# Value products of 64-feature heads over 128 columns, rings of PSUM banks begun anew in each stage, weaving words chosen anew

## The reference, cut to what matters

```python
def chunk_causal_softmax_attention(q, k, v, scale):          # 16 heads, v has 64 features
    ...
        sc = jnp.einsum('bhqd,bhkd->bhqk', qb, k).astype(jnp.float32) * scale
        sc = jnp.where(chunk_causal_mask(q_pos, k_pos), sc, -jnp.inf)
        p = jax.nn.softmax(sc, axis=-1)
        return jnp.einsum('bhqk,bhkd->bhqd', p.astype(v.dtype), v)

def stick_breaking_attention(q, k, v, scale):                # 8 heads of 64
    ...
        w = jnp.where(strict, jnp.exp(log_beta + later), 0.0)
        return jnp.einsum('bhqk,bhkd->bhqd', w.astype(v.dtype), v)

def _nsa_mixer(h, pos, pos_k, pos_v, wk1, wk2, wv1, wv2):    # 8 heads of 64, 2 groups of keys and values
    ...
    o_slc = _selected_attention(q, ks, vs, idx, pos)
    o_win = _window_attention(q, kw, vw)
    o = gt[..., 0:1] * o_cmp + gt[..., 1:2] * o_slc + gt[..., 2:3] * o_win
```

## Time and profile before

| | |
|---|---|
| median of three runs | 2344.5 us |
| the profiled execution: its own time, its span | 2355.76 us, 2354.0 us |
| ScalarE, GpSimd busy | 1109.1 us (47%), 421.9 us (18%) |
| TensorE weight loads busy | 1973.6 us (84%) |
| chain that ended last, share of TensorE | 89% |
| mean granted clock of TensorE | 0.969 |
| HBM | 306.89 MB read, 131 GB/s over the span |

### The profile page before, as it was taken

How to read it: one execution, slowest core, us unless ns; L and a number is a source line. 1 busy time by engine, 2 the same in 40 slices (tenths; PEclk the granted TensorE clock), 3 DMA queues, 4 the chain that set the end, 5 groups by cost and what they waited for, 6 DMA issues and landing times.

```text
span 2354.0 us, 36461 instructions
## 1 busy us (share of the span) xinstructions
PE 2240.2 (95%) x14254; PEld 1973.6 (84%) x14254; DVE 1534.3 (65%) x2717; ACT 1109.1 (47%) x2003; POOL 421.9 (18%) x377
## 2 busy tenths in 40 slices
PE   6999999999999999999999998999998898999997
PEld 5888889888888878998889886888888786788886
DVE  5976755587688668567765784457765675436765
ACT  4654454365465443535544333346544432235554
POOL 2421001122122100023200230002222140001223
PEclk9999999999999999999999999899998899879999
DMA  6554432255555543125544212124553311203552
GB/s 236 192 179 165 144 108 100 79 185 180 191 188 184 186 143 108 37 87 185 184 180 155 96 48 74 46 72 178 190 177 117 116 48 39 81 9 126 188 178 92
DMA packets 88732, 310.31 MB, mean 132 GB/s; under 512 B 9840, under 2 KB 12144, under 8 KB 88048
## 3 DMA queue, kind: packets, MB, share of 16 engines
q1 hardware_dynamic: 88272, 305.29, 36.6%
q10 hardware_dynamic: 288, 2.69, 0.3%
HBM read 306.89 MB, written 1.05 MB: 131 GB/s over the span
## 4 chain that ended last, share of the span: by engine, by line
PE 89%; DVE 5%; ACT 3%; issue 2%; POOL 1%; DMA 0%; SPq 0%; DVEq 0%; ACTq 0%; POOLq 0%
PE ps L140 87%; PE ps L145 2%; DVE scratch L165 2%; ACT scratch L154 1%; DVE w_lo L165 1%; ACT w_hi L154 1%; POOL scratch L165 1%; DVE x L165 0%; ACT scratch L191 0%; DVE scratch L192 0%; DVE stats L182 0%; DMA ring<-in_w 0%; ACT L159 0%; ACT h L154 0%; DVE scratch L177 0%
## 5 line engine op out<-in xcount | busy, mean ns | idle before, releaser
L165 DVE TENSOR_TENSOR w_lo<-ring,w_hi 128x1024 fp32r<-128x1024 f32 (+2 forms) x571 | 697.2, 1235 | 427.1 <-ACT w_hi L154 421.7
L140 PE MATMUL ps<-h,w_hi 128*128 128x512 f32 (+1 forms) x2784 | 871.6, 372 | 30.2 <-DVE h L177 19.1
L154 ACT ACTIVATE w_hi<-ring 128x1024 fp32r<-128x1024 f32 (+2 forms) x571 | 581.5, 1032 | 491.7 <-PE ps L140 484.9
L140 PE MATMUL ps<-h,w_lo 128*128 128x256 f32 x2448 | 687.8, 281 | 0.0
L140 PEld LDWEIGHTS ps<-h,w_hi 128*128 128x128 f32 x2784 | 505.7, 191 | 128.9 <-issue 26.6
L140 PEld LDWEIGHTS ps<-h,w_lo 128*128 128x128 f32 x2448 | 465.9, 190 | 0.0
L140 PE MATMUL ps<-f,w_hi 128*128 128x512 f32 (+1 forms) x1444 | 420.6, 357 | 2.6 <-DVE f L165 2.6
L140 PE MATMUL ps<-f,w_lo 128*128 128x256 f32 x1184 | 332.5, 281 | 0.0
L165 POOL TENSOR_TENSOR f<-f_work,f 128x256 fp32r<-128x256 f32 x132 | 188.2, 1426 | 598.0 <-ACT f L154 597.9
L140 PEld LDWEIGHTS ps<-f,w_hi 128*128 128x128 f32 x1444 | 256.3, 191 | 45.1 <-DVE w_lo L165 3.1
L140 PE MATMUL ps<-scratch 64*128 64x128 f32 (+10 forms) x1952 | 271.5, 311 | 18.1 <-DVE scratch L165 10.7
(11 more groups left out here) (136 smaller groups left out, 2223.8 us busy)
## 6 DMA issues: line engine op xcount, KB each, us to landing
ring<-in_w SPq DMA_DIRECT2D x520, 512.0 KB, 3.3
ring<-in_w SPq DMA_DIRECT2D x48, 384.0 KB, 3.5
ring<-in_w SPq DMA_DIRECT2D x16, 396.0 KB, 5.6
stage_consts<-in_ctwo ACTq DMA_DIRECT2D x1, 1344.0 KB, 5.8
stage_consts<-in_cthree ACTq DMA_DIRECT2D x1, 1281.0 KB, 5.4
ring<-in_w SPq DMA_DIRECT2D x9, 128.0 KB, 2.5
stage_consts<-in_cone SPq DMA_DIRECT2D x1, 1083.0 KB, 5.8
x<-in_x SPq DMA_DIRECT2D x4, 256.0 KB, 4.1
```

The source lines that it names most:

```text
L140: return self.e.matmul(out, lhsT, rhs, start=start, stop=stop, skip_group_check=free)
L154: return self.e.activation(out, x, func, **k)
L165: return self.e.tensor_tensor(out, a, b, op)
```

## The change

It has three parts.

1. The value products of heads with 64 features take 128 columns of values: the 64 that are wanted and 64 beside them (the other head of a pair, the other group, or the keys that lie next to the values). VectorE reads only the wanted half. This is in m0 (8 stick-breaking heads), m1, b0 and b1 (16 units each): 168 matmuls go from 128x64 to 128x128.
2. `K.cursor.clear()` at the start of each stage: every ring of banks begins at its first bank.
3. New words. Those of c0, c1, m0 and m1 are letter for letter as before. In b0 the 192 working pieces keep their order, two z are gone and a few have moved. In b1 the working pieces stand in another order, and there are 235 z where there were 252.

Of the dummies in the words, those issued are 230 in b0 (232 before), 217 in b1 (225) and 85 in c1 (91); in m0, m1 and c0 as many as before.

```diff
 WEAVE = {
...
-    "b1": ("zzzzzzzzzrrzzrgrrrhlrzzzzzrzzzzzzggzzhzzhzzzzzhrrhzzzhhzzzzzzzzzzzzzzzzzzzhzzzzhzzzzzzzzzrzhrzzh"
...
+    "b1": ("zzzzzzzzzrzrrrrzrgghzgrrhhhzlzzzzzzzzrzhzzzzzzzrhgzzhzhzzzzzzzzzzzrzzzzzrhhlrhzrzrzhrlzzzzzhhrzr"
...
 class Attn:
-    def __init__(self, K, name, lanes, q, k, v, dv, mask, bufs, stats, ready, values):
+    def __init__(self, K, name, lanes, q, k, v, dv, mask, bufs, stats, ready, values, col=None):
...
+        self.col = col or (lambda u: 0)
...
-                ins = e.mm(b[:, 256 * q:256 * q + A.dv], A.p(u)[:, c:c + 128], A.v(u, k), k == 0, k == n - 1)
+                ins = e.mm(b[:, 256 * q:256 * q + 128], A.p(u)[:, c:c + 128], A.v(u, k), k == 0, k == n - 1)
...
-            ins = sink(q, b[:, 256 * q:256 * q + A.dv], st[:, 4 + q:5 + q])
+            c = 256 * q + A.col(u)
+            ins = sink(q, b[:, c:c + A.dv], st[:, 4 + q:5 + q])
...
-        v = lambda k: T.vb[:, k, 64 * h:64 * h + 64]
+        v = lambda k: T.vb[:, k, 128 * (h // 2):128 * (h // 2) + 128]
...
-        e.mm(b[:, 0:64], l[:, 0:128], v(0), True, True)
+        e.mm(b[:, 0:128], l[:, 0:128], v(0), True, True)
...
-                      lambda u, k: self.c[:, k, 128 * u + 64:128 * u + 128], 64, "chunk", bufs,
+                      lambda u, k: self.c[:, k, 128 * u:128 * u + 128], 64, "chunk", bufs,
...
-                       lambda u, k: self.kk[:, k, 2 * (1 + u % 2) + 1, u // 8, :], 64,
+                       lambda u, k: self.kk[:, k, 2 * (1 + u % 2) + 1, :, :].rearrange("p g d -> p (g d)"), 64,
...
 def pe_program(e, K):
     e.wait_ge(K.S.sem("loaded_c"), 16)
     for name, T, order in stages(K):
+        K.cursor.clear()
         for what, i in order:
```

More of the change, by code:

```diff
@@ L40 @@
 WEAVE = {
[L41 to L45, removed]
-    "b1": ("zzzzzzzzzrrzzrgrrrhlrzzzzzrzzzzzzggzzhzzhzzzzzhrrhzzzhhzzzzzzzzzzzzzzzzzzzhzzzzhzzzzzzzzzrzhrzzh"
[L47 to L50, removed]
+    "b0": ("zzzzzzzzzzrrrrrrglrzzrzhgghhzhzzzzzzrzrhzzzzzzzzzzzzzzzzzhzzzzzzzzzzzzzhzzzzzzzzzzzzrhzzzzzzzhzh"
+           "rhhlzzzzzzrzzhrrhrgszzzzzzzhrzzzzhzshzzlhshrzszzhshrrhzznzzzzzzzzzzzzzzzzrzrzzzzzzzzzzzznzzznzzz"
+           "zzzzzzzznnzznznnrvzznrrrnzzzzrwzzzzzzszzrzzzzrnzzzzvwrzzzzzzzzzzszzzzzzzzzrzzznrzrsrnzursnuzrszz"
+           "zzzzrnnsuwvwsrsvsrurrrzwuzvzrururvzrvmwruwvuruvwrvwzrzvzzzuwzuuvzwvzuwwvuuwzvzumzwummmzzzzzmzzzz"
+           "zmmmmmmzzmzmmmzmmmmzzmzzzmzmmzmmzzzzzzzzzzmmmzzzzmzzmzzmzzmzzzzmmzz"),
+    "b1": ("zzzzzzzzzrzrrrrzrgghzgrrhhhzlzzzzzzzzrzhzzzzzzzrhgzzhzhzzzzzzzzzzzrzzzzzrhhlrhzrzrzhrlzzzzzhhrzr"
+           "zzzzzzzszzzzzzhzzzzzzhzrzrszzzrzhszzzhsshzrsrhrhzrzzhzzzzzzzzzzzszzzrzzzzzzzznzrzsznrsnrznzzzzzz"
+           "znzznzzwzrzzzzzznzzzznrzzsrzrnzrszrzzsrznwzzzzzzzzzzzzzzsrzzrzznvzzzzszzzzzzzzzzruzzzzzzzrzzznzz"
+           "znnrzvrnrnrwuzrurwurvuwvumrvuvrvzwrzzzzzzzzvuwuuzvwvuwwvuuwvvzuwwvuuzwzvumwummzmzmzzmmmmmmzzzmmz"
+           "zmmmzzmzmmmmmzzmmzmmzmzzmmzzzmzzmmzzzmzzmzz"),
     "c0": ("zzzzzzzzzpppzzzzpzzzzzzzzzzzzzzzzzzzzzzzzzzzzzzzzzzzzzzzzzzzpzpazcbacdbzacdbdozozzzozoozoozzozoo"
@@ L1555, in pe_stick @@
             e.wait_ge(*K.at("evicted", ((T.stage, "lvb"), t)))
-        e.mm(b[:, 0:64], l[:, 0:128], v(0), True, True)
-        e.mm(b[:, 256:320], l[:, 128:256], v(0), True, False)
-        e.mm(b[:, 256:320], l[:, 256:384], v(1), False, True).then_inc(*e.up("weighted", ("stick", h)))
+        e.mm(b[:, 0:128], l[:, 0:128], v(0), True, True)
+        e.mm(b[:, 256:384], l[:, 128:256], v(0), True, False)
+        e.mm(b[:, 256:384], l[:, 256:384], v(1), False, True).then_inc(*e.up("weighted", ("stick", h)))
 def act_mixer0(e, K, T, what, i):
@@ L1680, in dve_stick @@
         e.wait_ge(*K.at("weighted", ("stick", h)))
-        b = K.psum(("stick", h, "o"))[:, :].rearrange("p (t n) -> p t n", t=2)[:, :, 0:64]
+        b = K.psum(("stick", h, "o"))[:, :].rearrange("p (t n) -> p t n", t=2)[:, :, 64 * (h % 2):64 * (h % 2) + 64]
         e.cp(T.mix[:, :, 512 + 64 * h:576 + 64 * h], b).then_inc(*e.up("evicted", ("stick", h, "o")))
@@ L1726, in __init__ @@
         self.A = Attn(K, stage, 3, lambda u: self.qT[0:96, u, :], lambda u: self.kT[0:96, u, :],
-                      lambda u, k: self.c[:, k, 128 * u + 64:128 * u + 128], 64, "chunk", bufs,
+                      lambda u, k: self.c[:, k, 128 * u:128 * u + 128], 64, "chunk", bufs,
                       [K.st[:, 64 + 8 * i:72 + 8 * i] for i in range(3)],
-                      lambda u: [K.at("evicted", ((stage, n), u // 2)) for n in ("qT", "kT")], lambda u: [])
+                      lambda u: [K.at("evicted", ((stage, n), u // 2)) for n in ("qT", "kT")], lambda u: [], lambda u: 64)
     def chains(self):
@@ L2056, in __init__ @@
                        lambda u: self.kT[1 + u % 2][rows(u // 2), u // 8, :],
-                       lambda u, k: self.kk[:, k, 2 * (1 + u % 2) + 1, u // 8, :], 64,
+                       lambda u, k: self.kk[:, k, 2 * (1 + u % 2) + 1, :, :].rearrange("p g d -> p (g d)"), 64,
                        "causal", bufs, [K.st[:, 64 + 8 * i:72 + 8 * i] for i in range(3)],
                        lambda u: [K.at("evicted", ((stage, "nqT"), u // 8)), K.at("evicted", ((stage, "nkT", 1 + u % 2), 0))],
-                       lambda u: [])
+                       lambda u: [], lambda u: 64 * (u // 8))
     def block_of(self, what, i):
```

## The result

| | before | changed |
|---|---|---|
| median of the runs, on one chip | 2343.35 us | 2306.94 us |
| the profiled execution: its own time, its span | 2355.76 us, 2354.0 us | 2309.56 us, 2307.8 us |
| mean granted clock of TensorE | 0.969 | 0.980 |

The ratio of the runs is 0.9836, with a 95% interval of 0.9809 to 0.9863. The change is faster by 1.6%, about 38 us. One of the changed kernel's four executions took 7535.05 us at a mean granted clock of 0.369; it is in the median above but not in the ratio, and the median of the other three is 2304.33 us. The forecast was 2319.7 us with a range of 2306 to 2338: the direction was right, the gain was half as large again, and those three have their median just under the range.

A forecast was written before the change was run, and what follows sets the result against it. The prediction took TensorE, in its order and at the clock it is granted, as the bound. Its terms summed to -24.8 us, taken off the median of 2344.5 to give 2319.7 us, with a range from 2306 to 2338.

The forecast's parts named there:

- Value products, +3: 168 matmuls made twice as wide: nearly free but for group edges, a cost of 3 us.
- Rival 4: Value products: width sets the spacing, so they cost 19 us instead of 3; 2335.9 us, chance 0.05.
- Rings, -3.1, -2 and -0.7: Rings begun anew: f1's whole wait goes (-3.1 us), b0's start gains 2, six fewer dummies in c1 gain 0.7.
- The words, -8: b1's new order covers TensorE's 6.71 us wait for gate factors; 8 us saved, bounds -18 and +7.
- The clock in b1's last units, -11: Wide products end or prevent the 30 us at 1.2 GHz in b1's last attention units, saving 11 us.
- rival 1: b1's 30 us at low clock belong to the profiled execution alone; only -13.8, 2330.7 us, chance 0.22.
- The clock in b0, -3: In b0, 22 records at low clock: the clock rises earlier there, saving 3 us (0 and -5).
- f1's start: f1's first matmul was to follow c0's last dummy without idle time.
- b0's two pieces: The idle time before b0 was to be shorter than 3.68 us and broken in two.
- the 6.71: TensorE's 6.71 us wait for VectorE's gate factors in b1's first part, which was to go.

The follow-up runs named there:

- e19: The changed kernel measured once more, on another chip than its first runs: 2308.9 us.
- e1: The kernel before with the wide value products alone, rings and words as before: 2341.2 us.
- e8: The changed kernel with b1's new word used in b0 too, wide products: 2293.8 us.
- e13: Narrow value products, rings begun anew, and b1's new word in both b0 and b1: 2291.3 us.
- e11: e4's kernel with ring ATT starting one bank further at b1 (bank 4 first), as in the kernel before: 2335.2 us.
- e4: The changed kernel with the old word of b1: 2325.5 us.
- e2: The kernel before with the rings begun anew at each stage, narrow products and old words: 2347.0 us.
- e7: The kernel before with only ring ATT begun anew, at b1 alone: 2348.2 us.
- e5: e4's kernel with one letter of b1's old word moved, so that piece gl stands right behind gx: 2327.5 us.
- e10: The changed kernel with b1's new word up to piece gl and the old word from there on: 2322.9 us.
- e14: e10's kernel with the RWKV matrices and first inverse step of the first half of tokens ahead of the second half's: 2326.6 us.
- e15: e10's kernel with np2, the third product of the NSA projection, moved ahead of ge(3,1): 2322.7 us.
- e16: e10's kernel with the moves of e14 and e15 together: 2329.0 us.
- e6: The changed kernel with b1's new word up to the transpose nk0 and the old word from there on: 2311.3 us.
- e3: The kernel before with rings begun anew and b1's new word, narrow products and old b0 word: 2317.8 us.
- e17: The changed kernel with narrow value products, rings and both words as changed: 2320.2 us.
- e12: Narrow products, rings anew, new words, and 24 more dummies in each of b0's and b1's attention units: 2314.5 us.

## Why the prediction was right or wrong

The forecast had -24.8 us, the runs of the result have -38. The terms of the rings were right and the width cost less than its +3; two gains that the sum lacked or had too small brought some 21 us more, and two gains that it had, 14 us, did not come in the median. That the number was not farther off is in part luck: these errors had opposite signs.

The medians can be put in a row, each with one thing more (the first three on one chip, the last two on others, so that 2 us either way is not told apart there): wide products 2341.2, the rings without ATT's new place (and b0's new word) 2335.2, with it 2325.5, the new word of b1 2304.3 (the three runs of the result) and 2308.9 (e19).

**Value products, +3: right, small.** m1 went from 185.2 to 185.3 us and m0 from 184.8 to 185.1. e1 has the time of the executions of before at 0.974 or more, and e8 against e13 has 2.5 us for the whole width, which is not told apart from nothing. Rival 4 is out. Of the two rules of the Trainium skill ("TensorE: Matmul & The Clock Gate"), "LDWEIGHTS (loading the stationary operand)" has a load time that depends on the weight columns alone, so that the width would be free, and is near these numbers; "Back-to-back issue gap" has a formula for an isolated matmul from which some 9 us are estimated, and these numbers do not bear that out.

**Rings, -3.1, -2 and -0.7: right, but not all.** f1 lost 3.4 us with its whole wait. b0's idle time fell from 25.2 to 21.0 us and its length by 2.7; but in ten profiles with this b0 its length is 330.5 to 338.2 us, so the 2.7 is one draw of many, while the idle time is 20.7 to 21.5 in all ten. In c1 the sums of squares were not ready: 1.3 us of dummies became 0.9 of idle time. Rings without ATT's new place (and b0's new word) gave 6.0 us between e1 and e11, where I had 5.8. The first step that failed is the sentence "In f3, f5, m1 and the others TensorE's first bank was free in time: 0". It looks at first banks only. A stage also inherits how two rings that share banks stand to each other, here ATT (3 to 7) and that of the compression (4 to 7), and that decides two waits, 2.9 and 1.8 us, from 200 us into b1 on, and the clock around them. It is worth 9.7 us (e4 against e11), and e2, e7 and e11 show it in place.

**The words, -8: the mis-sized term, and the largest.** The word of b1 measured 17 to 21 us (e4 against the changed kernel). The prediction bounded the body of b1 by b0's at -18, and it came to -23.8 in the profile. Two causes are added up in that: width and rings, 6.2 us (290.1 to 283.9; with ATT's old place, in e11, it is 293.4), and the word, 17.6 (283.9 to 266.3). I valued the word by the one wait that it covers. e5 shows that covering it brings nothing; the new head alone brings 2.6 us (e10), and three rearrangements behind it bring nothing more (e14, e15, e16). The gain is in the whole order of the first part (e6), where idle time falls from 21.2 to 8.8 us; which of its places matter stays open. And b0 was no floor: under the same word it fell by 17.7 us itself (e8).

**The clock in b1's last units, -11: right in size in the profiled execution (11.9), wrong in the median.** Width alone ends that stretch (e1), so the cause given is a sufficient one; the new order with the rings anew ends it as well (e3), so it is not the only one. The error is in the frame: the sum was made against a profiled execution 11.3 us over the median, which is about what this stretch costs, and was then taken off the median. The runs of before on the result's chip took 2341.3 to 2345.0 us, the times of executions at 0.974 or more. Their clocks aren't on record, but by their times they had nothing to gain here, and rival 1 was right about this term. Where executions of lower clock are among the runs, as on the chip of e1, the term is there: e1 had 0.9962. In the result its absence was hidden by the ring phase and the word.

**The clock in b0, -3: wrong as stated, and the width's real worth.** b0's time at 1.2 GHz was 34.1 us before and 37.7 after; in the ten profiles with the new b0 it is 23.8 to 44.3, so neither a gain nor a loss is shown. But with the rings anew and narrow products it is 61.4 us (e2, e3 and e17), and b0 10 us longer. The width isn't shown to improve on the kernel before there; it keeps what the other edits would have lost. That is 11 to 16 us in the median (e17).

**What was said of the profile after.** f1's start, b0's two pieces, the 1.46 us in place of the 6.71, and the last units without a stretch came as written. b1 was to be between 335 and 350 us and was 329.3.

## What to carry to other kernels

Where banks or buffers come from rotating rings, list who held each one at every place, before and after, not only at a stage's start: a shift by one can make or end several waits far behind. An order for several in-order engines is not worth the wait that one move covers, since the moved step takes its weight splitting and evictions with it; try it in full, and try a good order in every stage that has the same pieces. Judge a gain in clock by the spread of many executions, since one profiled execution may be of either kind, and don't take a saving that was found in a slow profiled execution off a faster median; and look whether closing waits in one place brings a low stretch in another.

## What the runs showed of the hardware

**Short waits cost the clock, and closing them can cost it too.** With waits of 2.9 and 1.8 us more, the same pieces (492 records) took 74.11 us of TensorE at a clock of 0.87 and not 65.86 at 0.98 (before and e7). But e7 then runs 44.4 us at 1.2 GHz with TensorE busy throughout, and none of its twelve runs had a clock over 0.972, where 35 of 79 of before had. Why the clock falls there isn't shown. With wide products (e4) or 24 more dummies in b0 (e12) the stretches at these places were at most 10.2 and 13.7 us. With narrow products the long ones lasted 30.7 us (e2, e3, e17), 34.1 (before) and 44.4 (e2, e7), with TensorE busy all through them.

**Two paces at one granted clock.** A stage like f3 takes 187.8 us or 184.9, both at a granted clock of 1.00 and with TensorE busy throughout. f2 had 184.9 in all profiles. f3 had 184.9 in the changed kernel's first profile (shown above) and, with the same program, this in e19:

```profile
1063.30:1251.00 187.70, 187.70 (x1096) 164.29 (x1095) 137.44 (x221) 102.66 (x174) 33.47 (x26) 1.00 0.56 187
```

So the 3 us of f3 in the result belong to the execution and not to the change. The cause stays open.
